# The order of ScalarE and VectorE at the end of the experts, and six weight tiles behind the gather

## The reference, cut to what matters

```python
top_w, top_i = lax.top_k(e_prob, TOP_K)                  # two experts for each token
combine = one_hot(group) * in_group * g_w                # their weights
for g in range(N_GROUPS):
    a = einsum('td,edf->tef', t, w_gate[sl])
    u = einsum('td,edf->tef', t, w_up[sl])
    hid = silu(a) * u * combine[:, g, :, None]
    y = y + einsum('tef,efd->td', hid, w_down[sl])
x = x + gt2[:, None, :] * ffn
x = rms_norm(x, g_final)                                 # end of the first block
proj = einsum('bsd,de->bse', x, w_in[layer])             # start of the second
```

## Time and profile before

| | us |
|---|---|
| median of 3 runs | 1353.23 |
| lowest and highest | 1353.17, 1355.31 |
| the profiled execution's own time | 1354.75 |
| its span, first to last instruction | 1353.0 |
| TensorE busy in the span | 1254.0 (93%) |
| VectorE, ScalarE, POOL busy | 625.0, 461.8, 158.7 |

### The profile page before, as it was taken

The page is one execution under the profiler, slowest core; times in us unless marked ns, Lnnn a source line. Parts: engine busy times, 40 slices in busy tenths (PEclk is TensorE's granted clock), DMA queues, the critical chain, the costliest instruction groups (busy, mean ns, idle before and its releaser), DMA issues.

```text
span 1353.0 us, 17766 instructions
## 1 busy us (share of the span) xinstructions
PE 1254.0 (93%) x6976; PEld 891.0 (66%) x6976; DVE 625.0 (46%) x1131; ACT 461.8 (34%) x837; POOL 158.7 (12%) x126
## 2 busy tenths in 40 slices
PE   4899989999999889999889699999999999999996
PEld 1667556678887564454444278897556898787883
DVE  1654465554444353311111365324655745858544
ACT  3333236542222321111111251125564345555314
POOL 0200010000000000000000201602402056422000
PEclk9899999999999999999999799999999989999998
DMA  9565251023334369999999913321002312112301
GB/s 352 210 208 190 75 222 68 1 63 93 94 97 152 153 264 392 412 411 412 411 412 409 376 47 93 94 78 63 1 2 65 102 37 63 47 52 89 94 16 62
DMA packets 61633, 219.37 MB, mean 162 GB/s; under 512 B 6368, under 2 KB 6760, under 8 KB 61552
## 3 DMA queue, kind: packets, MB, share of 16 engines
q1 hardware_dynamic: 55440, 198.86, 40.3%
q10 hardware_dynamic: 3664, 10.47, 2.0%
q0 software_dynamic: 2448, 8.91, 1.7%
HBM read 203.52 MB, written 14.70 MB: 161 GB/s over the span
## 4 chain that ended last, share of the span: by engine, by line
PE 78%; DMA 8%; DVE 4%; ACT 4%; issue 4%; POOL 1%; SPq 0%; ACTq 0%; DVEq 0%; POOLq 0%
PE ps L639 12%; PE ps L640 12%; PE ps L641 12%; PE ps L926 6%; PE ps L907 4%; PE ps L735 3%; PE ps L947 3%; PE ps L758 3%; PE ps L745 3%; DMA ring<-in_w_moe 2%; PE ps L680 2%; PE ps L682 2%; PE ps L681 2%; PE ps L706 1%; DMA RG<-expert_rows,small 1%
## 5 line engine op out<-in xcount | busy, mean ns | idle before, releaser
L1615 DVE TENSOR_TENSOR ring_r<-ring,ring_r 128x1024 fp32r<-128x1024 f32 x115 | 145.8, 1271 | 206.3 <-ACT ring_r L1273 205.6
L1273 ACT ACTIVATE ring_r<-ring 128x1024 fp32r<-128x1024 f32 x116 | 121.2, 1053 | 204.4 <-PE ps L641 166.8
L639 PE MATMUL ps<-RB_r,ring_r 128*128 128x512 f32 x320 | 126.9, 396 | 1.1 <-DVE RH L1661 1.1
L641 PE MATMUL ps<-RB_r,ring_r 128*128 128x512 f32 x320 | 124.6, 389 | 0.0
L639 PE MATMUL ps<-RC_r,ring_r 128*128 128x512 f32 x224 | 91.2, 407 | 5.7 <-POOL RD_r L2380 4.7
L640 PE MATMUL ps<-RD_r,ring_r 128*128 128x512 f32 x224 | 88.0, 393 | 0.0
L641 PE MATMUL ps<-RC_r,ring_r 128*128 128x512 f32 x224 | 87.9, 392 | 0.0
L640 PE MATMUL ps<-RG_r,ring_r 128*128 128x512 f32 x208 | 81.1, 390 | 0.0
L926 PE MATMUL ps<-ring,RH 128*64 128x512 f32 x320 | 71.9, 594 | 0.0
L639 PEld LDWEIGHTS ps<-RB_r,ring_r 128*128 128x128 f32 x320 | 60.1, 188 | 16.7 <-issue 4.5
L907 PE MATMUL ps<-RD_r,RC_r 128*128 128x256 f32 x288 | 69.1, 296 | 1.2 <-DVE RD_r L1884 1.2
(11 more groups left out here) (438 smaller groups left out, 2620.3 us busy)
## 6 DMA issues: line engine op xcount, KB each, us to landing
ring<-in_w_moe SPq DMA_DIRECT2D x120, 512.0 KB, 15.6
ring<-in_w_post SPq DMA_DIRECT2D x68, 512.0 KB, 3.6
ring<-in_w_pre SPq DMA_DIRECT2D x48, 512.0 KB, 3.6
RE<-in_w_moe SPq DMA_DIRECT2D x44, 512.0 KB, 15.9
RF<-in_w_moe SPq DMA_DIRECT2D x40, 512.0 KB, 14.7
ring<-in_w_pre SPq DMA_DIRECT2D x16, 1024.0 KB, 7.0
expert_rows<-RD ACTq DMA_DIRECT2D x15, 512.0 KB, 6.9
ring<-in_w_pre SPq DMA_DIRECT2D x3, 2048.0 KB, 16.9
```

What stands on the lines that cost most here:

```text
L639: mm(out, part(m)[:, w], xh(k), start=first and k == 0, stop=False)
L641: ins = mm(out, remainder(m)[:, w], xh(k), start=False, stop=last and k == n_k - 1)
L1273: A(part(m), tile, ACT.Copy).then_inc(w_hi, 1)
L1615: v.tensor_tensor(remainder(m), arrival(m)[2], part(m).bitcast(F32), ALU.subtract).then_inc(w_split, 1)
```

## The change

ScalarE and VectorE take the work of the last pair ahead of most of the weighting of gathered rows, and SP holds six of the next stage's first eight weight tiles until both DMAs of the gather's last block have landed. No instruction is added or dropped on a compute engine.

```diff
@@ SP
             for n in range(N_POST):
-                if n < 4:
+                if n < 2:
                     sp.wait_ge(moe_used, N_FIRST + 8 + n_over * PAIR_TILES)
                 elif n < RING:
                     sp.wait_ge(moe_used, N_FIRST + 16 + n_over * PAIR_TILES)
+                    sp.wait_ge(g_in[TT - 1], 32)
@@ ScalarE
-            weighted(0)
-            weighted(1)
             gate(last_p + 1, N_FIRST + 16 + n_over * PAIR_TILES, last_p + n_over)
-            weighted(2)
             act.wait_ge(late_ok, 1)
             downs_split(last_p, N_FIRST + 20 + n_over * PAIR_TILES, n_over)
             turned_hidden(last_p + 1, N_FIRST, n_over)
-            weighted(3)
             hi(M_Q2)
+            weighted(0)
             downs_split(last_p + 1, N_FIRST + 24 + n_over * PAIR_TILES, n_over)
             hi(M_Q2 + 1)
+            for t in range(1, TT):
+                weighted(t)
@@ VectorE
-            top_two(0)
-            top_two(1)
             hidden(last_p + 1, last_p + n_over, n_over)
-            top_two(2)
             late_rest(last_p, 0)
             late_rest(last_p, 1)
-            top_two(3)
-            lo(M_Q2)
+            top_two(0)
             late_rest(last_p + 1, 0)
             late_rest(last_p + 1, 1)
+            lo(M_Q2)
+            for t in range(1, TT):
+                top_two(t)
```

## The result

| | before | changed |
|---|---|---|
| median, us | 1354.91 (20 runs) | 1359.48 (20 runs) |
| lowest and highest | 1352.23, 1360.59 | 1356.60, 1362.14 |
| ratio | | 1.003, interval 1.002 to 1.004 |
| profiled execution: span | 1353.0 | 1357.1 |

The forecast was 1354.0, within 1352.0 to 1356.2, and within 0.2% of before. The change costs 4.6 us, which is outside the range and slower by over 0.2%. Of the 5.5 us between 1354.0 and 1359.48, 1.7 us are the base: the forecast stood on a median of three runs (1353.23), and the median of twenty is 1354.91.

What follows compares the result with a forecast made beforehand. The prediction took the gather's last landing to set the end around the change. An earlier feature_rows start (-0.6 us) plus a cold start (+1.4) gave +0.8 us, so 1354.0 from a 1353.23 median, range 1352.0 to 1356.2.

Steps and rivals of the forecast that it cites:

- What bounds the kernel now: Around the change, the gather's last landing at 771.40 us sets the end, leading to TensorE's first feature_rows at 775.78.
- The gather lands 1.6 us sooner: With six tiles deferred, the gather's last DMA lands at 769.8 instead of 771.4 us; bounds 0 and 1.6.
- `hi(M_Q2)` holds ScalarE until its tile lands: ScalarE reaches the first next-stage split at 758 and stands until its tile lands at 765.6 us, ahead of all weighted.
- the forecast's own row: ScalarE's and VectorE's work in sequence from the first new tile's landing at 765.6 to feature_rows at about 775.2 us.
- The second `down` takes 5.15 us: On TensorE, down(last_p + 1) starts at 763.1 when its last tile lands, runs at half clock and ends at 768.25.
- Cold start, +1.4: TensorE stands 7.0 us before feature_rows, so the first one runs at half clock, costing 1.4 us.
- the bound of +2.5: Upper bound of the cold-start cost at feature_rows, in us, if the clock stays at half for 6.8 us.
- The sum: An earlier feature_rows start, -0.6 us, plus its cold start, +1.4, gives +0.8 us for the whole change.
- The slower one: TensorE stays at half clock 8 us or more from 775.2; net +2.5 us and up, 1355.8 to 1357; 14 in 100.
- The faster one: New tiles land early and the second down runs warm, giving 1351.7 us; 8 in 100 for over 0.2%.
- The deferral does nothing: The gather alone runs no faster than its half share and lands at 771.4 as before; time still 1354.0; no separate chance.

Runs made afterwards that it cites:

- Weighting first: Changed kernel with all four weighted ahead of both next-stage splits and the last down's evictions, top_two likewise on VectorE; ratio to before 0.9987 with the deferral, 0.9994 without.

## Why the prediction was wrong

**What bounds the kernel now: right.** The gather sets the end. Its last landing is at 25.8 us in all five traces of before, and `feature_rows` starts at 30.2 in four of them. In the fifth it is the third block, through a second `down` of 6.60 us at half clock, that ends last, at 30.4. `split_two` follows at a fixed distance of 4.97 us.

**The gather lands 1.6 us sooner: sized too high, without effect.** In the changed trace it lands 0.6 us sooner (25.3 instead of 25.8), because SP's queue ran empty later. As forecast, nothing hung on it, and no engine waited for a deferred tile.

**`hi(M_Q2)` holds ScalarE until its tile lands: right as a mechanism, mis-sized by 3.8 us.** This is the step that failed. I took the landings of one trace (763.1 and 765.6) as a property of the kernel. They are the end of a queue whose backlog at the gather's start differs between executions (with TensorE's clock in one `down` before it, as shown above), and which drains at half rate from there on, so that each microsecond of backlog comes out as two. In before this number has no effect, so its times gave no warning. The change replaced an end that is steady, the gather's, by one that isn't, and the trace I had showed it near its best: 17.5, of 15.9 to 21.9 in the fifteen traces of the table. I had the page's total and the landing, and never asked what would happen if the queue stood one or two tiles further back. With the tile 4.1 us later (24.2 instead of 20.0 after the gather's first issue) the forecast's own row gives 33.8 instead of 29.6.

**The second `down` takes 5.15 us: it took 6.34.** The clock was at half for all but its last microsecond. Because it also began 3.9 us later, ScalarE's second `hi` and three `weighted` hung on its end: 34.8 instead of 33.8. That branch stands in the prediction's row (`downs_split` at 768.3, `hi` at 768.9), where it held ScalarE up by 0.7 us.

**Cold start, +1.4: right.** `feature_rows` to `split_two` took 6.2 us instead of 4.97, +1.2. In the second trace it took 7.0 us, +2.0, with the clock at half until 786, within the bound of +2.5. The Trainium skill's page TensorE: Matmul & The Clock Gate (section What's actually happening) says that the point of change varies from run to run of the same kernel. The traces agree: the second `down` of the unchanged kernel took 5.02, 5.15, 5.32, 5.47 and 6.60 us.

**The sum.** -0.6 + 1.4 became +4.6 + 1.2 = +5.8 us from before to the changed trace at `split_two` (35.2 to 41.0). The medians differ by 4.6. The difference of 1.2 isn't resolved by single traces: what follows `split_two` took 571.5 to 575.3 us in the five traces of before and 570.9 and 572.4 in the two of the changed kernel.

**The rivals.** The slower one was the right side for a different reason: I gave it to the clock alone, with a chance of 14 in 100. The rival that was missing is "the new end is later in other executions than in this one". The faster one failed as argued. "The deferral does nothing" was wrong for a kernel that still waits for the gather: alone it is worth 0.17% (0.06 to 0.28).

**Better than both:** the deferral alone, 0.9983 of before (1352.92 us). Weighting first with the deferral is 0.9987. The two can't be told apart.

## What to carry to other kernels

Before moving a wait in front of work on an in-order engine, ask how steady the thing is that it waits for: a landing at the end of a shared queue that nobody waited for can differ by microseconds from one execution to the next, while the times of the kernel show nothing of it. Two or three traces of the same kernel begin to show the spread: here five traces of one kernel cover all of it. And when an order and a deferral go together, time them apart: here one gained 0.17% and the other lost 0.22%.

## What the runs showed of the hardware

- Two queues with work share the DMA engines evenly, 50 and 56 packets in one microsecond in the earlier trace rows, and gather blocks land 5.12 us apart with SP's queue busy and 2.49 us apart without. DMA: Bandwidth & Descriptors (the Trainium skill, section Queues, rings and completion order) says that each DMA engine takes its queues in turn by packet; the traces agree, with 0.20 MB each in a microsecond. What I hadn't drawn from it is the other side: what a queue has left when a second one starts takes twice as long. The gather's first bytes come some 4.3 us after its first issue (in the kernel before between 749 and 750 us, the row below), so the landings at 15.9 to 21.9 us stand for an estimated 6 to 9 us of work at the full rate behind that point ((15.9 - 4.3) / 2 and (21.9 - 4.3) / 2).

```profile
q0 software_dynamic: 11, 0.05, 11.1%
```

- The same sixteen multiplications of `down` took between 3.65 and 6.60 us, by how much of them fell into the half clock.
- With the same work and the same waits ahead of it, the clock fell within a `down` in four of fifteen traces and stayed full in eleven (5.35 against 3.65 us). 1.7 us on TensorE came out as some 4 us at the landing of SP's last down tile, counted from the gather's first issue (means 17.0 and 21.0), where 3.4 would follow from the halved rate.
- What is left of the spread stays open in part. In four traces (landings at 15.9, 16.8, 19.6 and 20.1) the clock also fell in the `down` two before that one, which took 5.10 to 5.35 us, and in one (20.1) that earlier `down` waited 3.19 us for its tile, where it is 1.6 to 3.0 in the others.
